# Two neighbouring rows of w_down per partition, and transposes that read every second column

## The chip, the cores and the metric

The kernel runs on one core of a Trainium2 chip. The metric is the device time of one execution in microseconds (us). Engines are named as the profile names them: PE is TensorE's matmul stream and PEld its weight loads, DVE is VectorE, ACT is ScalarE, POOL is GpSimd, SP is SyncE, which here only issues transfers.

## The reference, cut to what matters

The block takes 512 tokens of width 1024 through a mixer (differential attention beside gated linear attention), a cross attention over 256 memory rows, and a mixture of 32 experts with 4 experts a token. All data are float32. The change touches the experts alone:

```python
def expert_block(args):
    xb, e = args
    u = xb @ w_up[e] + b_up[e]
    glu = jnp.minimum(u[:, :D_FF], SWIGLU_LIMIT)
    lin = jnp.clip(u[:, D_FF:], -SWIGLU_LIMIT, SWIGLU_LIMIT)
    act = glu * jax.nn.sigmoid(SWIGLU_ALPHA * glu) * (lin + 1.0)
    return act @ w_down[e] + b_down[e]
```

`D_FF` is 1024, so `w_up[e]` is 1024 x 2048 (8 MB) and `w_down[e]` is 1024 x 1024 (4 MB). The product with `w_down` is a sum over 1024 rows, and its order is free.

## The kernel before

The dense stages come first (a list of steps, `plan_steps`), then the 32 experts. An expert works on up to 96 token slots: group A of 64 and group B of 32. Token rows are gathered from HBM by POOL (lines 530 and 533), transposed by `rows_T` (lines 803 and 805), multiplied with `w_up` in `up_pair` (line 835), put through SwiGLU by DVE and ACT (`swiglu`, `gates`), transposed again by `hidden_T` (lines 813 and 816), multiplied with `w_down` in `down` (line 863 for group A, line 872 for group B), and added to the output rows in HBM by two scatters of POOL (lines 541 and 547).

**Weights.** Every weight goes through `ring`, six slots of 1 MB (8 KB on each of the 128 partitions). SP alone fills it, in a fixed order: in the loop over experts `load_up` issues the eight chunks of the next expert's `w_up`, then `load_down` the four chunks of this expert's `w_down`. A slot is refilled when PE has counted `chunk_used` up for the chunk that it held. Chunk c of `w_up` is rows 128c to 128c+127, row 128c+p on partition p: 8 KB in one piece. Chunk c of `w_down` is two blocks of 128 rows, row 256c+p and row 256c+128+p on partition p: two pieces of 4 KB that lie 512 KB apart in HBM. `down` reads the chunk as two halves, `u` = 0 and 1, each with the transposed activations of index k = 2c+u as weights.

**Activations.** `actA` and `actB` hold the SwiGLU result, 512 columns on each partition. A slot's first 512 features are on one partition and its last 512 on another, so a transpose of 128 columns gives two of the eight indices k. `hidden_T` takes 128 neighbouring columns at a time, as the stationary operand of the transpose (the identity is streamed), into PSUM banks 5 and 6; from there ACT (line 1103) and DVE (line 1473) copy them into `hTA` and `hTB`.

**Order.** PE's order in the loop body of expert i is fixed by the code: the bias of the next expert's up projection (line 824), its chunks 0 and 1, `hidden_T(i)`, `index`, chunks 2 to 7, `rows_T(i+2)`, `down(i)`. Two experts are thus always under way, and DVE and ACT do SwiGLU beside `down`.

Of the kernel before, what the change touches and what calls it, by code (L numbers as in the profile page):

```python
# [14 lines left out]
P = 128  # L15
# [86 lines left out]
def decoder_block(nc, A, slots=SLOTS):  # L102
# [33 lines left out]
    with ExitStack() as ctx:  # L136
        def sb(name, shape, dt=F32):
            return ctx.enter_context(nc.sbuf_tensor(name, shape, dt))

        def sem(name):  # L140
            return ctx.enter_context(nc.semaphore(name))

        bank = [ctx.enter_context(nc.psum_tensor(f"bank{b}", [P, 512], F32)) for b in range(8)]
# [3 lines left out]
        ring_flat = ring.rearrange("p s k n -> p s (k n)")  # L147
# [12 lines left out]
        ident = sb("ident", [P, P])  # L160
# [79 lines left out]
        assert at[0] <= at_gla  # L240
        actT_w = actT.rearrange("p k n -> p (k n)")
        gluA, linA, sigA, actA, gluB, linB, sigB, actB = [actT_w[:, HD * q:HD * q + HD] for q in range(8)]

        sp = [0]

# [24 lines left out]
        chunk_in = [sem(f"chunk_in{s}") for s in range(RING)]  # L270
# [61 lines left out]
        def ps(job):  # L332
            return bank[job_at[job][0]]
# [9 lines left out]
        def ready(eng, job):  # L343
            b, k = job_at[job]
            eng.wait_ge(bank_full[b], k + 1)
# [31 lines left out]
        def up_chunk(e, c):  # L377
            return A["w_up"][0][e, P * c:P * c + P, :]

        def down_chunk(e, c):  # L380
            return A["w_down"][0].rearrange("e (k p) n -> e p k n", p=P)[e, :, 2 * c:2 * c + 2, :]

        slot_dense = [16 * len(range(s, DENSE, RING)) for s in range(RING)]
        def expert_chunk_in(eng, q, o):
# [10 lines left out]
        @block.sync  # L395
        def _(sp_):
            chunk = 0
            for name, g in groups:
                for half in range(2):
                    src = A["w_in"] if name in first_col else A[square[name]]  # L400
                    c0 = first_col[name] if name in first_col else 512 * g
                    if chunk >= RING:
                        ready(sp_, group_jobs[groups[(chunk - RING) // 2]])
                    w = src[0].rearrange("(k p) n -> p k n", p=P)[:, 4 * half:4 * half + 4, c0:c0 + 512]
                    sp_.dma_start(ring[:, chunk % RING, :, :], w).then_inc(chunk_in[chunk % RING], 16)
                    chunk += 1
            ready(sp_, group_jobs[groups[-1]])
            sp_.sem_inc(chunk_used, RING)

            def load_up(q, o, e):  # L410
                for c in range(UP_CHUNKS):
                    sp_.wait_ge(chunk_used, q * PER_EXPERT + (o + c + 1))
                    slot = (o + c) % RING
                    sp_.dma_start(ring_flat[:, slot, :], up_chunk(e, c)).then_inc(chunk_in[slot], 16)

            def load_down(q, o, e):
                for c in range(DOWN_CHUNKS):
                    sp_.wait_ge(chunk_used, q * PER_EXPERT + (o + c + 1))
                    slot = (o + c) % RING
                    sp_.dma_start(ring_flat[:, slot, :].rearrange("p (k n) -> p k n", k=2), down_chunk(e, c)).then_inc(chunk_in[slot], 16)  # L420

            load_up(0, 0, 0)
            with sp_.Fori(0, NE - 1) as i:
                load_up(i, UP_CHUNKS, i + 1)
                load_down(i, UP_CHUNKS + UP_CHUNKS, i)
            load_down(NE - 1, UP_CHUNKS, NE - 1)
            sp_.wait_ge(table_ready, 1)
            extra = sp_.value_load(ovf[0:1, 2 * MO:2 * MO + 1], min_val=0, max_val=MO)
            with sp_.If(extra > 0):
                with sp_.Fori(0, extra) as m:  # L430
                    e = sp_.value_load(ovf[0:1, bass.ds(m, 1)], min_val=0, max_val=NE - 1)
                    load_up(m + NE, 0, e)
                    load_down(m + NE, UP_CHUNKS, e)
            for b in range(NB):
                sp_.wait_ge(fin_ready, b + 1)
                sp_.dma_start(A["out"][0, P * b:P * b + P, :], x_res[:, b, :]).then_inc(out_done, 16)
            sp_.wait_ge(out_done, 16 * NB)
# [139 lines left out]
        def _(pe):  # L577
# [38 lines left out]
            for s in steps:  # L616
# [7 lines left out]
                elif kind == "norm":  # L624
                    n = NORMS[s[1]][0]
                    pe.wait_ge(xn_ready, NB * (n + 1))
                    for k in range(KT):
                        begin(pe, s + (k,))
                        for b in range(NB):
                            t = pe.transpose(ps(s + (k,))[:, P * b:P * b + P], tokA[:, b, P * k:P * k + P], ident[:, :])  # L630
                        finish(t, s + (k,))
                elif kind == "norm_mem":
                    pe.wait_ge(memn_ready, MB)
                    for k in range(0, KT, 2):
                        begin(pe, s + (k,))
                        for k2 in range(2):
                            for b in range(MB):
                                t = pe.transpose(ps(s + (k,))[:, M * k2 + P * b:M * k2 + P * b + P],
                                                 mem_x[:, b, P * (k + k2):P * (k + k2) + P], ident[:, :])
# [5 lines left out]
                elif kind == "qkT":  # L645
                    pe.wait_ge(roped, s[1] + 1)
                    begin(pe, s)
                    for b in range(NB):
                        c0 = 512 * s[1] + P * s[2]
                        t = pe.transpose(ps(s)[:, P * b:P * b + P], tokA[:, b, c0:c0 + P], ident[:, :])  # L650
# [11 lines left out]
                elif kind == "scores":  # L662
                    h, i = s[1] // 4, s[1] % 4
# [7 lines left out]
                elif kind == "attnT":  # L671
                    n, i = s[1], s[1] % 4
                    pe.wait_ge(a_ready, n + 1)
                    begin(pe, s)
                    for j in range(i + 1):
                        t = pe.transpose(ps(s)[:, P * j:P * j + P], abuf[:, n % 2, P * j:P * j + P], ident[:, :])
                    finish(t, s)
                elif kind == "attnV":
                    n, h, i = s[1], s[1] // 4, s[1] % 4
# [7 lines left out]
                elif kind == "gla_scores":  # L687
                    c, t = s[1], s[2]
# [9 lines left out]
                elif kind == "gla_kd":  # L698
                    c, t = s[1], s[2]
                    begin(pe, s)  # L700
                    finish(pe.transpose(ps(s)[:, 0:P], gqkT[:, 2 + t, P * c:P * c + P], ident[:, :]), s)
                elif kind == "gla_out":
                    c, t = s[1], s[2]
# [15 lines left out]
                elif kind == "gla_state":  # L719
                    c, t = s[1], s[2]  # L720
# [4 lines left out]
                elif kind == "oT":  # L725
                    pe.wait_ge(mixed_ready, NB)
                    for k in range(KT):
                        begin(pe, s + (k,))
                        for b in range(NB):
                            t = pe.transpose(ps(s + (k,))[:, P * b:P * b + P], tokA[:, b, P * k:P * k + P], ident[:, :])  # L730
                        finish(t, s + (k,))
                elif kind == "xscores":
                    h, i = s[1], s[2]
# [7 lines left out]
                elif kind == "xT":  # L741
# [3 lines left out]
                    for i in range(NB):  # L745
                        t = pe.transpose(ps(s)[:, P * i:P * i + P], xp[:, h % 2, i, P * mb:P * mb + P], ident[:, :])
# [11 lines left out]
                elif kind == "router":  # L758
# [10 lines left out]
                    for b in range(NB):  # L769
                        t = pe.transpose(ps(j)[:, NE * b:NE * b + NE], lgT[:, P * b:P * b + P], ident[0:NE, 0:NE])  # L770
# [37 lines left out]
            def hidden_T(n):  # L808

                pe.wait_ge(actA_ready, n + 1)  # L810
                pe.wait_ge(actB_ready, n + 1)
                for i in range(KT // 2):
                    t = pe.transpose(bank[5][:, P * i:P * i + P], actA[:, P * i:P * i + P], ident[:, :])  # L813
                t.then_inc(hTA_done, 1)
                for i in range(KT // 2):
                    t = pe.transpose(bank[6][:, 64 * i:64 * i + 64], actB[0:64, P * i:P * i + P], ident[0:64, 0:64])  # L816
                t.then_inc(hTB_done, 1)

            def up_bias(n):
# [68 lines left out]
            with pe.Fori(0, NE - 1) as i:  # L888
                up_bias(i + 1)
                pe.wait_ge(xTA_ready, i + 2)  # L890
                pe.wait_ge(xTB_ready, i + 2)
                up_pair(i, UP_CHUNKS, 0)
                hidden_T(i)
                pe.wait_ge(idx_ready, 2 * i + 4)
                index(i + 2, i + 2)
                for pair in range(1, KT // 2):
                    up_pair(i, UP_CHUNKS, pair)
                pe.wait_ge(hTA_ready, i + 1)
                pe.wait_ge(hTB_ready, i + 1)
                rows_T(i + 2)  # L900
                down(i, i, 2 * UP_CHUNKS)
            pe.wait_ge(xTA_ready, NE + 1)
            pe.wait_ge(xTB_ready, NE + 1)
            hidden_T(NE - 1)
            down(NE - 1, NE - 1, UP_CHUNKS)
            pe.wait_ge(table_ready, 1)
            extra = pe.value_load(ovf[0:1, 2 * MO:2 * MO + 1], min_val=0, max_val=MO)
            with pe.If(extra > 0):
                with pe.Fori(0, extra) as m:
                    e = pe.value_load(ovf[0:1, bass.ds(m, 1)], min_val=0, max_val=NE - 1)  # L910
                    index(m + (NE + 1), e)
                    rows_T(m + (NE + 1))
                    up_bias(m + NE)
                    pe.wait_ge(xTA_ready, m + (NE + 2))
                    pe.wait_ge(xTB_ready, m + (NE + 2))
                    for pair in range(KT // 2):
                        up_pair(m + NE, 0, pair)
                    hidden_T(m + NE)
                    down(m + NE, m + NE, UP_CHUNKS)
# [658 lines left out]
```

## Time and profile before

| | us |
|---|---|
| median of 3 runs | 1800.74 (1798.44 to 1803.96) |
| profiled execution | 1798.54 |
| its span, first to last instruction | 1796.7 |
| dense stages and router, to about 640 | 640 |
| start of the first expert, to 727 | 87 |
| experts at a steady pace, 727 to 1749 | 1022 |
| last product, scatters, final norm, output | 48 |
| mean granted clock of PE, share of full speed | 0.965 |

The span is what the trace shows; the profiled execution took 1.8 us more around it. Busy shares over the whole span mix stages with different limits, so the views below are read by stretch. PE's ends are modelled from a pipeline: a row's mean duration overlaps with its neighbours, and the pace of PE is read from the chain of waits.

### The profile page before, as it was taken

What the parts mean: (1) busy time and instruction counts of PE and PEld (TensorE: products, weight loads), DVE (VectorE), ACT (ScalarE), POOL (GpSimd) and SP (SyncE); (2) the same over time, 40 slices, a digit from 0 to 9 for tenths busy, and PEclk for the clock granted to TensorE, in tenths of its full rate; (3) what the DMA queues carried; (4) which work ended last, traced back from release to release, by engine and by line L of the source; (5) the groups of instructions that cost most, each with busy time, mean ns of one, the idle gap of its engine ahead of it and who ended that gap; (6) DMA issues with size and microseconds to landing.
All of it is one profiled execution on the core that took longest, in us unless ns stands there. A gap on an engine that the chain in (4) does not pass through costs nothing.

```text
span 1796.7 us, 31195 instructions
## 1 busy us (share of the span) xinstructions
PE 1632.7 (91%) x12187; PEld 743.7 (41%) x12188; DVE 533.8 (30%) x1388; ACT 283.1 (16%) x561; POOL 211.4 (12%) x202
## 2 busy tenths in 40 slices
PE   3995979978999758999999999999999999999992
PEld 2442437543454313444434434444443443444441
DVE  2012464221031243223224223323322422322331
ACT  3013324211130201001101101100100110110113
POOL 1000000051000110111121121121111112112111
PEclk9998989989999879999999999999999999999996
DMA  6121111223100557999999999999999999999993
GB/s 213 47 94 47 47 47 48 94 77 105 47 1 0 228 185 309 367 380 387 379 355 401 382 364 390 385 369 384 381 376 381 377 394 364 389 389 369 390 360 107
DMA packets 105522, 467.49 MB, mean 260 GB/s; under 512 B 14062, under 2 KB 14114, under 8 KB 72624
## 3 DMA queue, kind: packets, MB, share of 16 engines
q1 hardware_dynamic: 89152, 438.33, 62.2%
q0 software_dynamic: 13744, 25.46, 5.9%
q10 hardware_dynamic: 2592, 3.25, 0.5%
q8 instruction: 20, 0.33, 0.1%
q14 instruction: 14, 0.11, 0.0%
HBM read 456.89 MB, written 18.87 MB: 265 GB/s over the span
## 4 chain that ended last, share of the span: by engine, by line
PE 86%; DVE 6%; ACT 4%; issue 2%; ACTq 1%; DMA 1%; POOL 0%; DVEq 0%; POOLq 0%
PE bank L835 37%; PE bank L613 20%; PE bank L863 12%; PE bank L872 6%; PE bank L824 1%; PE bank L803 1%; PE bank L813 1%; PE bank L755 1%; DVE arena L1269 1%; PE bank L630 1%; PE bank L805 1%; PE bank L816 1%; ACT L945 1%; PE bank L850 1%; ACT L946 1%
## 5 line engine op out<-in xcount | busy, mean ns | idle before, releaser
L835 PE MATMUL bank<-ring,arena 128*32 128x512 f32 x6144 | 679.2, 594 | 0.0
L835 PEld LDWEIGHTS bank<-ring,arena 128*32 128x32 f32 x6144 | 227.7, 110 | 402.6 <-issue 335.5
L863 PE MATMUL bank<-ring,arena 128*32 128x512 f32 x2048 | 267.8, 592 | 0.0
L613 PE MATMUL bank<-ring,actT 128*128 128x512 f32 x576 | 252.0, 597 | 1.9 <-DVEq L355 1.9
L1450 DVE TENSOR_SCALAR actT<-bank 64x512 f32<-64x512 f32 x64 | 43.7, 683 | 435.1 <-PE bank L835 434.1
L613 PEld LDWEIGHTS bank<-ring,actT 128*128 128x128 f32 x576 | 109.3, 192 | 137.7 <-issue 134.5
L872 PE MATMUL bank<-ring,arena 128*32 128x512 f32 x1024 | 157.9, 592 | 0.0
L863 PEld LDWEIGHTS bank<-ring,arena 128*32 128x32 f32 x2048 | 112.8, 110 | 96.2
L530 POOL DMA_INDIRECT arena<-h_rows,arena x33 | 35.1, 1062 | 901.3 <-DVE arena L1434 901.3
L1097 ACT ACTIVATE actT<-actT 128x512 f32<-128x512 f32 x32 | 20.2, 630 | 526.2 <-DVE actT L1450 526.2
L613 PE MATMUL bank<-actT,ring 128*128 128x512 f32 x192 | 82.8, 593 | 1.2 <-DVEq L355 1.2
L872 PEld LDWEIGHTS bank<-ring,arena 128*32 128x32 f32 x1024 | 58.1, 110 | 51.7
L1480 DVE SCALAR_TENSOR_TENSOR arena<-bank,arena 64x512 f32<-64x512 f32 x32 | 23.8, 743 | 152.0 <-ACT arena L1111 152.0
L1109 ACT ACTIVATE arena<-bank,arena 128x512 f32<-128x512 f32 x32 | 22.0, 687 | 230.6 <-PE bank L863 230.6
L1473 DVE COPY arena<-bank 128x256 f32<-128x256 f32 x32 | 13.5, 423 | 150.6 <-PE bank L816 150.6
L541 POOL DMA_INDIRECT acc_rows<-arena x32 | 51.7, 1615 | 40.4 <-ACT arena L1109 20.0
L613 PEld LDWEIGHTS bank<-actT,ring 128*128 128x128 f32 x192 | 36.4, 190 | 46.9 <-issue 45.4
L547 POOL DMA_INDIRECT acc_rows<-arena x32 | 46.6, 1457 | 9.8 <-issue 9.8
L1103 ACT ACTIVATE arena<-bank 128x512 f32<-128x512 f32 x32 | 19.1, 597 | 178.0 <-PE bank L813 178.0
L630 PE MATMUL bank<-ident,tokA 128*128 128x128 f32 x96 | 16.7, 356 | 31.4 <-DVE tokA L1169 21.1
L1452 DVE TENSOR_SCALAR actT<-bank 64x512 f32<-64x512 f32 x64 | 44.4, 694 | 1.4
L493 POOL DMA_DIRECT2D abuf<-in_w_router x1 | 1.1, 1067 | 368.9 <-DVE tokA L1336 368.9
(284 smaller groups left out, 1308.8 us busy)
## 6 DMA issues: line engine op xcount, KB each, us to landing
ring<-in_w_up SPq DMA_DIRECT2D x256, 1024.0 KB, 6.5
ring<-in_w_down SPq DMA_DIRECT2D x128, 1024.0 KB, 7.8
ring<-in_w_in SPq DMA_DIRECT2D x12, 1024.0 KB, 8.2
ring<-in_w_ck SPq DMA_DIRECT2D x4, 1024.0 KB, 5.6
ring<-in_w_cv SPq DMA_DIRECT2D x4, 1024.0 KB, 6.2
ring<-in_w_out SPq DMA_DIRECT2D x4, 1024.0 KB, 5.7
ring<-in_w_cq SPq DMA_DIRECT2D x4, 1024.0 KB, 6.1
ring<-in_w_co SPq DMA_DIRECT2D x4, 1024.0 KB, 6.3
```

Source lines behind the costliest of these rows:

```text
L530: g.indirect_dma_start(out=xgA[:, :], out_offset=None, in_=h_rows, in_offset=bass.IndirectOffsetOnAxis(ap=idxA_next[:, :], axis=0), bounds ...
L541: g.indirect_dma_start(out=acc_rows, in_=yA[:, :], out_offset=bass.IndirectOffsetOnAxis(ap=idxA_cur[:, :], axis=0), in_offset=None, bounds ...
L547: g.indirect_dma_start(out=acc_rows, in_=yB[0:2 * NARROW, :], out_offset=bass.IndirectOffsetOnAxis(ap=idxB_cur[0:2 * NARROW, :], axis=0), ...
L613: mm = pe.matmul(o, lhsT, rhs, start=(k == 0), stop=(k == KT - 1))
L630: t = pe.transpose(ps(s + (k,))[:, P * b:P * b + P], tokA[:, b, P * k:P * k + P], ident[:, :])
L835: mm = pe.matmul(bank[g][32 * t:32 * t + 32, :], lhsT, w[:, 512 * t:512 * t + 512], start=False, stop=(k == KT - 1))
L863: mm = pe.matmul(bank[3][r:r + 32, :], hTA[:, k % 4, g, k // 4, :], w[:, 512 * t:512 * t + 512], start=False, stop=(k == KT - 1))
L872: mm = pe.matmul(bank[4][r:r + 32, :], hTB[:, k % 4, k // 4, :], w[:, 512 * t:512 * t + 512], start=(k == 1), stop=(k >= KT - 2))
L1109: a.activation(yA, bank[3][:, :], ACT.Copy, scale=gateA_tab[:, bass.ds(col, 1)]).then_inc(yA_ready, 1)
L1450: v.tensor_scalar(gluA[64 * g:64 * g + 64, :], bank[g][0:64, :], LIMIT, None, ALU.min).then_inc(gluA_ready, 1)
L1452: ins = v.tensor_scalar(linA[64 * g:64 * g + 64, :], bank[g][64:128, :], LIMIT, -LIMIT, ALU.min, ALU.max)
L1480: v.scalar_tensor_tensor(out=yB[0:64, :], in0=bank[4][0:64, :], scalar=gateB_tab[0:64, bass.ds(col, 1)], in1=yB_odd[0:64, :], op0=ALU.mult ...
```

## The change

Two things change together. First, chunk c of `w_down` becomes rows 256c to 256c+255 with rows 256c+2p and 256c+2p+1 on partition p. These lie next to each other in HBM, so each partition's 8 KB is one piece, and the transfer's pattern is 128 x 2048 in place of 128 x 2 x 1024. The slot's half `u` then holds the rows 256c+2p+u. Second, the transposes of `hidden_T` must bring the matching features to partition p: index k = 2c+u now needs features 256c+2n+u for n from 0 to 127, which are every second column of a block of 256. The view `actA_u` names them; transpose i reads block i // 2, parity i % 2, with a step of two columns (8 bytes). What the transposes write, the copies after them and the loops of `down` are as they were. No instruction is added, removed or moved on any engine: the five engines' programs have as many rows as before, in the same order.

```diff
         gluA, linA, sigA, actA, gluB, linB, sigB, actB = [actT_w[:, HD * q:HD * q + HD] for q in range(8)]
+        actA_u, actB_u = [t_.rearrange("p (c n u) -> p c n u", n=P, u=2) for t_ in (actA, actB)]
...
         def down_chunk(e, c):
-            return A["w_down"][0].rearrange("e (k p) n -> e p k n", p=P)[e, :, 2 * c:2 * c + 2, :]
+            return A["w_down"][0].rearrange("e (c p u) n -> e c p (u n)", p=P, u=2)[e, c, :, :]
...
                     slot = (o + c) % RING
-                    sp_.dma_start(ring_flat[:, slot, :].rearrange("p (k n) -> p k n", k=2), down_chunk(e, c)).then_inc(chunk_in[slot], 16)
+                    sp_.dma_start(ring_flat[:, slot, :], down_chunk(e, c)).then_inc(chunk_in[slot], 16)
...
                 for i in range(KT // 2):
-                    t = pe.transpose(bank[5][:, P * i:P * i + P], actA[:, P * i:P * i + P], ident[:, :])
+                    t = pe.transpose(bank[5][:, P * i:P * i + P], actA_u[:, i // 2, :, i % 2], ident[:, :])
                 t.then_inc(hTA_done, 1)
                 for i in range(KT // 2):
-                    t = pe.transpose(bank[6][:, 64 * i:64 * i + 64], actB[0:64, P * i:P * i + P], ident[0:64, 0:64])
+                    t = pe.transpose(bank[6][:, 64 * i:64 * i + 64], actB_u[0:64, i // 2, :, i % 2], ident[0:64, 0:64])
                 t.then_inc(hTB_done, 1)
```

## Rows read from the trace of the kernel before

**Rows 1.** Busy time by stretch: us, then engines, granted clock, DMA share, GB/s.

```profile
0.00:640.00 640.00, 524.37 (x1611) 273.36 (x1612) 177.63 (x432) 146.05 (x343) 42.80 (x68) 0.94 0.22 77
640.00:727.00 87.00, 74.24 (x686) 27.71 (x690) 29.39 (x94) 7.93 (x12) 8.52 (x9) 0.89 0.74 283
727.00:1749.00 1022.00, 1022.00 (x9784) 436.21 (x9776) 319.43 (x854) 109.75 (x178) 151.86 (x118) 1.00 0.99 380
1749.00:1797.00 48.00, 12.11 (x114) 6.44 (x110) 7.33 (x10) 19.37 (x29) 8.27 (x8) 0.66 0.33 103
```

**Rows 2.** All that PE waited for from 645: total us, times, longest.

```profile
PE bank L824 <- DVE arena L1442: 6.1, 1, 6.1
PE bank L803 <- DMA arena<-h_rows,arena: 6.1, 1, 6.1
PE bank L850 <- DVE arena L1473: 1.2, 1, 1.2
```

**Rows 3.** SP's waits from 645, and SP's issues around 1000 (start, us).

```profile
SPq L420 <- PE bank L835: 287.6, 126, 3.3
SPq L414 <- PE bank L872: 286.5, 120, 3.5
...
1000.97 8.09 SPq L420 DMA_DIRECT2D ring<-in_w_down  x4
1011.29 20.54 SPq L414 DMA_DIRECT2D ring<-in_w_up  x8
1035.43 8.09 SPq L420 DMA_DIRECT2D ring<-in_w_down  x4
```

**Rows 4.** Chain of waits inside one expert's body: start, us, what ran.

```profile
893.39 0.58 PE bank L813 x4
893.98 0.39 PE bank L816 x4
894.37 0.19 PE bank L794 x4
894.55 0.10 PE bank L796 x4
894.65 15.59 PE bank L835 x144
...
927.85 0.59 PE bank L813 x4
```

**Rows 5.** Transfers to landing: the page's medians; L420 alone, 727 to 1700.

```profile
ring<-in_w_up SPq DMA_DIRECT2D x256, 1024.0 KB, 6.5
ring<-in_w_down SPq DMA_DIRECT2D x128, 1024.0 KB, 7.8
...
DMA to landing us min/median/max: 5.6/7.8/9.9
```

**Rows 6.** Packets over the whole span, from the page.

```profile
DMA packets 105522, 467.49 MB, mean 260 GB/s; under 512 B 14062, under 2 KB 14114, under 8 KB 72624
q1 hardware_dynamic: 89152, 438.33, 62.2%
```

**Rows 7.** Packets of queue q1 (SP): 1010.5 to 1013.5, then 1016 to 1022.

```profile
q1 hardware_dynamic: 323, 1.25, 102.0%
...
q1 hardware_dynamic: 343, 2.55, 101.7%
```

**Rows 8.** Lines 813, 816, 613: duration in ns, min/median/max, and shapes.

```profile
L813 PEld LDWEIGHTS bank<-ident,actT x128: 137/140/145, 686.5 to 1749.4; 128*128 128x128 f32 x128
L816 PEld LDWEIGHTS bank<-ident,actT x128: 135/138/141, 687.1 to 1749.9; 64*128 64x128 f32 x128
L613 PEld LDWEIGHTS bank<-ring,arena x64: 186/190/192, 324.5 to 358.8; 128*128 128x128 f32 x64
```

**Rows 9.** Passes of 512 columns: dense stage (line 613), experts (line 835).

```profile
L613 PE MATMUL bank<-ring,actT x576: 592/592/1057, 35.2 to 601.5; 128*128 128x512 f32 x192
L835 PE MATMUL bank<-ring,arena x6144: 591/592/1062, 650.2 to 1736.8; 128*32 128x512 f32 x199
```

## The prediction

> **What bounds the kernel now.** I read the busy time by stretch first, because the change lies wholly in the expert loop. From 727 to 1749 PE is busy for 1022.00 of 1022.00 us at the full granted clock (1.00, the 2.4 GHz level) [rows 1]. In the same stretch the DMA engines are at a share of 0.99 and move 380 GB/s. So two resources look full, and the question for this change, which helps one of them, is which one sets the pace.
>
> The waits answer it. From 645 on PE waited three times in all, 6.1, 6.1 and 1.2 us, for a weight selector, for the first gather of token rows, and for one copy of transposed activations at the very end [rows 2]. Not one wait is on a chunk of the ring, so PE never stood still for a weight. The other side of the ring tells the same: SP waits for PE 126 times before a `w_down` chunk (287.6 us) and 120 times before a `w_up` chunk behind `down` (286.5 us) [rows 3]. It is the full ring that holds SP back. The pace confirms it: SP's four `w_down` issues begin at 1000.97 and the next four at 1035.43, a period of 34.46 us [rows 3], and the transposes of line 813 begin at 893.39 and at 927.85 in the chain of waits, again 34.46 us [rows 4]. Both follow PE's own list of instructions. The DMA share of 0.99 says that packets are under way, not that anybody waits for them.
>
> **The margin of a chunk.** A slot is freed when PE ends a chunk and is needed again six chunks later, so at least five chunks of PE work lie between. Six chunks of the up projection take 15.59 us in the chain [rows 4], 2.60 each, so five are 13.0 us. `w_down` chunks land after 7.8 us at the median and 9.9 us at the worst [rows 5]. The worst one still has 3.1 us to spare, the typical one 5.2 us.
>
> **Part one, the transfers.** 128 transfers change (32 experts, 4 chunks). In each, 256 packets of 4 KB become 128 of 8 KB. That takes 128 x 128 = 16384 packets off queue q1, which had 89152, and off the total of 105522; the packets under 8 KB, 72624 of them, lose all 32768 of `w_down` [rows 6].
>
> What a packet costs I take from two stretches in which q1 moves nearly one kind only. From 1010.5 to 1013.5 it moves 1.25 MB, 305 pieces of 4 KB, at a share of 102.0% of 16 engines x 3 us: 49.0 us, or 160 ns a piece. From 1016 to 1022 it moves 2.55 MB, 311 pieces of 8 KB, at 101.7% of 96 us: 97.6 us, or 314 ns [rows 7]. Two small ones cost 320 ns, one large one 314: 6 ns gained. An engine gets 8 of the large pieces of a chunk, so a chunk saves about 50 ns and the kernel 128 x 8 x 6 ns = 6.1 us of DMA time. Bounds: none of it, or all of it. All of it would need the DMA to set the pace; it does not [rows 2, 3]. A landing of 7.8 us that became 7.7, or even the 6.5 us of `w_up` [rows 5], is further inside a margin that is never used. I take 0 us. The cover is PE's own work, 34.46 us for an expert. It is not thick: the twelve chunks of an expert take each DMA engine 64 pieces of 314 ns and 64 of 160 ns, 30.3 us, and the gathers and scatters come on top. If PE were some 3 us an expert faster, the 6.1 us would begin to count.
>
> The Trainium skill, Perfetto Trace Analysis, section DMA Optimizations, says that larger transfers saturate HBM better and can "dramatically improve throughput", from 2 KB to 4 or 8 KB, and ties this to a kernel that is DMA-bound. By that rule, with its condition left aside, this would be a gain. The packets of rows 7 differ by 2% per byte, and the condition is not met.
>
> Could the new pattern be slower? `w_up` is fetched today with just this pattern, 128 x 2048 with 8 KB a partition and 1 MB in one piece, and lands sooner, at 6.5 us [rows 5]. That excludes a loss worth a term. The issue itself, on SP, lies in a wait for PE. The gathers and scatters share the engines with this queue, and nothing in the steady loop waits for them [rows 2].
>
> **Part two, the transposes.** 8 transposes an expert now load a stationary operand whose columns stand 8 bytes apart: 256 loads in all, 128 on line 813 and 128 on line 816 [rows 8]. These lie on the path, since PE is the bound. The writes to PSUM and the copies behind them are unchanged.
>
> No row of this trace shows a strided load by PE, so the cost is bounded. First, how much of a load is on the path? Four transposes of line 813 take 0.58 us in the chain and four of line 816 0.39 us [rows 4], 145 and 98 ns each. They differ by 64 streamed columns, so 64 columns are worth 47 ns and 128 columns 94 ns. Some 50 ns of each transpose is thus not streaming; it is of the kind that a slower load would lengthen. So I do not count on a hidden load: what a load grows by, PE loses.
>
> The lower bound is 0: each load stays at 140 ns and 138 ns. I see no way below zero, as no column is saved. A middle value is the slower kind of load of the same shape that the trace has: 128x128 float32 for an ordinary matmul takes 190 ns against 140 for the transposes [rows 8], 50 ns more. 256 x 50 ns = 12.8 us. The upper bound is a load that doubles outright: 256 x 139 ns = 35.6 us. I take 0 us. The nearest rows are those of the same loads; the operand has the same number of columns and the same partitions, and each is a single 4-byte word per partition either way.
>
> The Trainium skill, Advanced Engine Details and Errata, section Memory Cachelines, says that SBUF is read in lines of 16 bytes and that at least two accesses must hit a line to hide the memory's latency. At 8 bytes apart two of the wanted words lie in each line where four did, so by that rule the cost is nothing, but this is its last free step; if the rule were off by one hit, the slower case below would hold. No run here shows it yet.
>
> **The sum.** Transfers 0, transposes 0, everything else untouched: 1798.5 us for an execution like the profiled one (span 1796.7 and 1.8 around it). That execution was 2.2 us under the median of the three runs, and nothing in the change removes that spread, so the forecast for the median is the median before, 1800.7 us.
>
> **The rivals.**
>
> *Strided loads cost (slower).* The place is lines 813 and 816; the price is the growth of a load times 256. Against it: same column count. For it: no strided load in the trace, and loads that are not hidden. With the middle value it gives 1800.7 + 12.8 = 1813.5 us, with the upper bound 1836.3 us. It is decisive from 21 ns a load (5.4 us, 0.3%).
>
> *The DMA is the bound after all (faster).* For it: the share of 0.99. Against it: no wait of PE on the ring. A second way to gain would be that DMA writes slow PE's reads; but a pass of 512 columns takes 592 ns in the dense stage, at a DMA share of 0.22, and 592 ns among the experts at 0.99 [rows 1, 9]. In full this rival gives 1800.7 - 6.1 = 1794.6 us.
>
> *The packets do not change.* If the pattern were cut into 4 KB pieces anyway, the count on q1 would stay at 89152, and the time would still be 1800.7 us, since the transfers are hidden. `w_up` speaks against it: the packets of 8 KB and over are 105522 - 72624 = 32898 [rows 6], which is 256 x 128 of `w_up` and a few more.
>
> **How the numbers follow.** Forecast (with the packets changed) 0.74; packets unchanged, same time, 0.03; strided loads at about 50 ns 0.12; strided loads nearer to doubling 0.05, which leaves a little for loads that grow by less than 21 ns in the first case; DMA gain 0.06. Within 0.3% is about what a measurement of this kernel can tell from no change, 5.4 us here. That gives faster 0.05 (the DMA gain's price is just past the limit, so a part of it stays within), same 0.78, slower 0.17. The range goes from the DMA gain, 1794.6, to the middle price of the strided loads, 1813.5 with half a microsecond for scatter; it leaves out the doubling and half of what lies around 1813.5.
>
> **What the profile after would show.** Right: q1 at 72768 packets (89152 - 16384), packets under 8 KB at 39856 (72624 - 32768), loads of lines 813 and 816 still at 140 and 138 ns, the four transposes at 0.58 and 0.39 us in the chain, the period of SP's `w_down` issues at 34.46 us, no wait of PE on the ring, `w_down` landing between 6.5 and 7.8 us. Wrong on the slow side: loads of 813 and 816 at 160 ns or more, and a period longer by eight times the growth, 0.40 us at 50 ns. Wrong on the fast side: a period under 34.46 us with the same PE instructions, which would mean that PE's pace hung on the DMA in a way that the waits do not show.

## The result: 10 us slower, all of it in the transposes

The changed kernel takes 1809.33 us (median of 7 runs, 1807.85 to 1814.31); the kernel before, timed beside it, takes 1799.13 us (7 runs, 1798.3 to 1804.09). The ratio is 1.0056 with a 95% interval from 1.0039 to 1.0073: slower, by 10.2 us. The time lies inside the range that was given, but the forecast was no change, and that was wrong.

The stretches of the kernel after, as in [rows 1]:

```profile
0.00:640.00 640.00, 530.24 (x1611) 277.37 (x1612) 173.51 (x412) 146.16 (x343) 41.71 (x65) 0.94 0.22 77
640.00:727.00 87.00, 69.14 (x630) 26.23 (x630) 32.22 (x104) 7.33 (x11) 7.74 (x9) 0.86 0.69 263
727.00:1749.00 1022.00, 1022.00 (x9700) 442.20 (x9702) 313.69 (x850) 108.25 (x175) 153.99 (x120) 1.00 0.98 376
1749.00:1812.00 63.00, 27.54 (x256) 13.72 (x248) 14.58 (x23) 21.60 (x32) 8.28 (x8) 0.74 0.48 174
```

PE is still busy for all of the steady stretch, at the full clock, but it gets through 9700 instructions where it did 9784 [rows 1]. It has become slower at its own work; nothing has come to stand in its way. What it waited for from 645 on, as in [rows 2], names no chunk of the ring. The wait of 7.1 us is not new: the kernel before has it too (7.13 us, ending at 640.5), and here it falls behind 645 because this execution is some 5 us later at that point. SP waits for PE before `w_down` chunks a little longer than before (302.0 us against 287.6, [rows 3]):

```profile
PE bank L795 <- DVE arena L1421: 7.1, 1, 7.1
PE bank L825 <- DVE arena L1443: 6.2, 1, 6.2
PE bank L804 <- DMA arena<-h_rows,arena: 6.1, 1, 6.1
PE bank L851 <- DVE arena L1474: 0.8, 1, 0.8
...
SPq L421 <- PE bank L836: 302.0, 126, 3.6
```

The lines after 240 stand one higher than before: 814 and 817 are the transposes of `hidden_T`, 804 and 806 those of `rows_T`, 836 is the up projection. SP's issues give the period (start, us), and the chain of waits through one body (start, us, what ran) gives the place, to be laid beside [rows 3] and [rows 4]:

```profile
904.95 8.05 SPq L421 DMA_DIRECT2D ring<-in_w_down  x4
...
939.74 8.05 SPq L421 DMA_DIRECT2D ring<-in_w_down  x4
```

```profile
900.44 0.68 PE bank L814 x4
901.12 0.62 PE bank L817 x4
901.74 0.19 PE bank L795 x4
901.93 0.10 PE bank L797 x4
902.03 15.59 PE bank L836 x144
917.62 0.59 PE bank L804 x4
918.21 0.39 PE bank L806 x4
```

The period is 34.79 us in place of 34.46, 0.33 us more. The four transposes of group A went from 0.58 to 0.68 us and the four of group B from 0.39 to 0.62, which is 0.33 us too. The up projection is at 15.59 us as before, and the transposes of `rows_T`, which were not touched, at 0.59 and 0.39. 32 experts times 0.33 us are 10.6 us; 10.2 were measured. Thirty periods together, from SP's first group of `w_down` issues to its 31st, took 1033.95 us before (690.79 to 1724.74) and 1043.61 us after (696.23 to 1739.84): 9.66 us more, 0.322 a period, 10.3 us in 32 experts. The weight loads behind it, as in [rows 8] (ns, min/median/max):

```profile
L814 PEld LDWEIGHTS bank<-ident,actT x128: 194/209/223, 691.6 to 1764.6; 128*128 128x128 f32 x128
L817 PEld LDWEIGHTS bank<-ident,actT x128: 191/213/220, 692.3 to 1765.3; 64*128 64x128 f32 x128
...
L804 PEld LDWEIGHTS bank<-ident,arena x132: 138/140/230, 652.1 to 1752.7; 128*128 128x128 f32 x132
```

The strided loads take 209 and 213 ns where they took 140 and 138; the loads of line 804 stay at 140. The other half of the change did what it says (packets, as in [rows 6], and landings, as in [rows 5]):

```profile
DMA packets 89139, 467.49 MB, mean 258 GB/s; under 512 B 14063, under 2 KB 14115, under 8 KB 39857
q1 hardware_dynamic: 72768, 438.33, 61.7%
...
ring<-in_w_up SPq DMA_DIRECT2D x256, 1024.0 KB, 6.8
ring<-in_w_down SPq DMA_DIRECT2D x128, 1024.0 KB, 7.0
```

The profiled execution of the kernel after, 1813.64 us, is 15.1 us over the profiled one of before. Some 5 us of that lie ahead of the experts: line 804 begins at 652.1 us, line 803 of before at 647.0. PE's granted clock differs there (from 170 to 300 it is 0.88 of full speed after, 0.91 before), and executions of either kernel differ by so much among themselves, 1798.3 to 1804.1 us before and 1807.9 to 1814.3 after. The experiments are therefore read by the period in the steady stretch, and their medians beside it.

### The profile page after: what moved, and what is told of

Read it like the earlier page. It is cut to its first block, busy times and chain, and to the rows that moved or that the text cites. A ratio compares the mean times of both kernels' runs of the same rounds, so it can differ in the third digit from the quotient of the medians.

```text
span 1811.9 us, 31195 instructions
## 1 busy us (share of the span) xinstructions
PE 1648.9 (91%) x12187; PEld 759.5 (42%) x12188; DVE 534.0 (29%) x1388; ACT 283.3 (16%) x561; POOL 211.7 (12%) x202
## 2 busy tenths in 40 slices
DMA packets 89139, 467.49 MB, mean 258 GB/s; under 512 B 14063, under 2 KB 14115, under 8 KB 39857
## 3 DMA queue, kind: packets, MB, share of 16 engines
q1 hardware_dynamic: 72768, 438.33, 61.7%
## 4 chain that ended last, share of the span: by engine, by line
PE 86%; DVE 6%; ACT 4%; issue 2%; ACTq 1%; DMA 1%; POOL 0%; DVEq 0%; POOLq 0%
PE bank L836 37%; PE bank L614 20%; PE bank L864 12%; PE bank L873 6%; PE bank L825 1%; PE bank L814 1%; PE bank L804 1%; PE bank L817 1%; PE bank L756 1%; PE bank L631 1%; DVE arena L1270 1%; PE bank L806 1%; ACT L946 1%; PE bank L851 1%; ACT L947 1%
```

## The experiments

Two theories stood after the result. Theory L: the strided weight loads are the whole loss. Rival D: the 8 KB pieces cost something, with the longer loads only beside it. The first four kernels undo one part each, move the cost to another engine, and double it. "The kernel before" ran beside each set.

### The transfers alone

```diff
# against the changed kernel
-                    t = pe.transpose(bank[5][:, P * i:P * i + P], actA_u[:, i // 2, :, i % 2], ident[:, :])
+                    t = pe.transpose(bank[5][:, P * i:P * i + P], actA[:, P * i:P * i + P], ident[:, :])
...
-                    t = pe.transpose(bank[6][:, 64 * i:64 * i + 64], actB_u[0:64, i // 2, :, i % 2], ident[0:64, 0:64])
+                    t = pe.transpose(bank[6][:, 64 * i:64 * i + 64], actB[0:64, P * i:P * i + P], ident[0:64, 0:64])
```

> Only the transfers change: each partition's 8 KB of a w_down chunk is one piece, the transposes read neighbouring columns as before. (The features meet the wrong rows of w_down, so the sum over the 1024 features is paired wrongly; the work is the same.) Theory L, the strided weight loads are the whole loss: the time of before, 1799 us within 3, a period of 34.46 us for SP's w_down issues, no wait of PE on the ring, w_down landing at about 7.0 us in place of 7.8. Rival D, the 8 KB pieces disturb something (gathers, the dense stages that ended 5 us later in the profile after): about 1809 us, with lines 813 and 816 at 140 and 138 ns.

1799.37 us against 1799.38, ratio 1.0004 (0.9995 to 1.0014). The `w_down` issues start 34.47 us apart here, and thirty periods take 1033.94 us where the kernel before took 1033.95:

```profile
828.70 8.05 SPq L421 DMA_DIRECT2D ring<-in_w_down  x4
...
863.17 8.05 SPq L421 DMA_DIRECT2D ring<-in_w_down  x4
```

The loads of both lines are back at 140 and 138 ns. The 8 KB pieces cost nothing and bring nothing here. One item of the expectation missed: `w_down` landed after 8.5 us at the median (5.2 to 10.4), not sooner than the 7.8 of before. Even 10.4 us is under the 13 us after which the slot is read.

### The strided transposes alone

```diff
# against the kernel before
+        actA_u, actB_u = [t_.rearrange("p (c n u) -> p c n u", n=P, u=2) for t_ in (actA, actB)]
...
-                    t = pe.transpose(bank[5][:, P * i:P * i + P], actA[:, P * i:P * i + P], ident[:, :])
+                    t = pe.transpose(bank[5][:, P * i:P * i + P], actA_u[:, i // 2, :, i % 2], ident[:, :])
...
-                    t = pe.transpose(bank[6][:, 64 * i:64 * i + 64], actB[0:64, P * i:P * i + P], ident[0:64, 0:64])
+                    t = pe.transpose(bank[6][:, 64 * i:64 * i + 64], actB_u[0:64, i // 2, :, i % 2], ident[0:64, 0:64])
```

> Only the transposes change: they read every second column, the transfers are two pieces of 4 KB as before. (The features meet the wrong rows of w_down; the work is the same.) Theory L: the time of after, 1809.5 us within 3; weight loads of the two transposes at about 209 and 213 ns, four transposes at 0.68 and 0.62 us in the chain, a period of 34.79 us. Rival D: 1799 us.

1810.29 us against 1799.38, ratio 1.0059 (1.0044 to 1.0074). The period is 34.79 us (832.53 to 867.32 in SP's issues), the chain has 0.68 and 0.62 us for the two fours. The whole loss is here, with the old transfers. Theory L holds and rival D falls.

### The same pairing with the step moved to DVE

```diff
# against the changed kernel
-        actA_u, actB_u = [t_.rearrange("p (c n u) -> p c n u", n=P, u=2) for t_ in (actA, actB)]
+        actA_o, actB_o = [t_.rearrange("p (c u n) -> p c u n", n=P, u=2) for t_ in (actA, actB)]
+        linA_u, sigA_u, linB_u, sigB_u = [t_.rearrange("p (c n u) -> p c u n", n=P, u=2) for t_ in (linA, sigA, linB, sigB)]
...
-                v.tensor_tensor(actA, linA, sigA, ALU.mult).then_inc(actA_ready, 1)
+                v.tensor_tensor(actA_o, linA_u, sigA_u, ALU.mult).then_inc(actA_ready, 1)
...
-                v.tensor_tensor(actB[0:64, :], linB[0:64, :], sigB[0:64, :], ALU.mult).then_inc(actB_ready, 1)
+                v.tensor_tensor(actB_o[0:64], linB_u[0:64], sigB_u[0:64], ALU.mult).then_inc(actB_ready, 1)
```

The transposes read `actA` and `actB` 128 neighbouring columns at a time again.

> The whole change, but DVE's last product of SwiGLU reads its operands with a step of two columns and writes them in the order that the transposes want, so that every weight load reads neighbouring columns. The result is that of the changed kernel. Theory L: 1799 us within 3, the period back at 34.46 us, DVE's two products perhaps longer than 0.69 us (a step of 8 bytes) but hidden, since actB is ready about 10 us before hidden_T. Rival D: 1809 us. If DVE's strided reads doubled its two products, the 1.4 us an expert would still be hidden.

1800.0 us against 1799.38, ratio 1.0006 (0.9996 to 1.0017): this kernel computes what the changed kernel computes, with its 8 KB pieces, in the time of the kernel before. DVE's groups by shape (busy us, mean ns):

```profile
L1464 DVE TENSOR_TENSOR actT<-actT 128x512 f32<-128x512 f32 x32 | 23.9, 748 | 1.1
L1471 DVE TENSOR_TENSOR actT<-actT 64x512 f32<-64x512 f32 x32 | 23.4, 730 | 0.0
```

The two products, which read both operands with a step of two columns, take 748 and 730 ns. In the kernel before the same two products (lines 1462 and 1469) took 692 and 673 ns. DVE pays 56 and 57 ns for 512 columns, once each an expert, on an engine that is not the bound.

### The suspected cost doubled

```diff
# against the changed kernel
+        xgA_u, xgB_u = [t_.rearrange("p (c n u) -> p c n u", n=P, u=2) for t_ in (xgA, xgB)]
...
-                    pe.transpose(bank[5][:, P * i:P * i + P], xgA[:, P * i:P * i + P], ident[:, :])
+                    pe.transpose(bank[5][:, P * i:P * i + P], xgA_u[:, i // 2, :, i % 2], ident[:, :])
...
-                    t = pe.transpose(bank[6][:, 64 * i:64 * i + 64], xgB[0:64, P * i:P * i + P], ident[0:64, 0:64])
+                    t = pe.transpose(bank[6][:, 64 * i:64 * i + 64], xgB_u[0:64, i // 2, :, i % 2], ident[0:64, 0:64])
```

> The suspected cost doubled: the changed kernel, whose transposes of the gathered token rows (rows_T, lines 804 and 806 of the changed kernel) also read every second column. (The token features then meet the wrong rows of w_up; the work is the same.) Theory L: another 0.33 us an expert, 1.0 to 1.1 us for the 33 pairs in all 10.8 us more than the changed kernel: about 1820 us, 21 us over the kernel before, loads of lines 804 and 806 (here one line lower) at about 209 and 213 ns. Rival D: no more than the changed kernel, 1809 us.

1824.2 us against 1799.38 (4 runs, 1820.57 to 1826.44), ratio 1.0131 (1.0112 to 1.0151): 24.8 us over the kernel before where 21 were expected. The period is 35.11 us (812.64 to 847.75 in SP's `w_up` issues), 0.65 over 34.46, which is twice 0.33 and makes 20.8 us in 32 experts. Where the remaining 4 us between the medians lie is not shown. The profiled execution reaches the first transposes of token rows at 653.7 us, 6.7 later than the profiled one of before, and this later start does not come with the step: the kernels with steps of three and four columns, further down, issue their first `w_down` chunk at 691.5 and 691.9 us, the kernel before at 690.8. The fastest runs of the two kernels are 22.7 us apart.

### One group at a time, and wider steps

The load grew by about 70 ns, but a transpose of group A only by about 23 and one of group B by about 58. Two kernels take the step away from one group each.

```diff
# stride_a, against the changed kernel: only group B's transposes are put back
-                    t = pe.transpose(bank[6][:, 64 * i:64 * i + 64], actB_u[0:64, i // 2, :, i % 2], ident[0:64, 0:64])
+                    t = pe.transpose(bank[6][:, 64 * i:64 * i + 64], actB[0:64, P * i:P * i + P], ident[0:64, 0:64])
```

> Only the four transposes of group A (128 streamed columns) read every second column, those of group B read neighbours. (Group B's features meet the wrong rows of w_down; the work is the same.) Theory C, the stream covers a part of a longer load: the load grows by 69 ns but the transpose by 24 to 26 only, four of them 0.68 us in place of 0.59, a period of 34.55 us, about 3 us over the kernel before. Rival S, each group's growth came partly from the other group's loads queued beside it: the four A transposes and the four B transposes would then share 0.33 us in another way, and this kernel would cost about half of it, 5 us.

> Only the four transposes of group B (64 streamed columns) read every second column. (Group A's features meet the wrong rows of w_down; the work is the same.) Theory C: four of them 0.62 us in place of 0.39, a period of 34.69 us, about 7.5 us over the kernel before. Rival S: about 5 us.

The second kernel puts back group A's in the same way. The chains of the two, A's first:

```profile
929.33 0.68 PE bank L814 x4
930.01 0.39 PE bank L817 x4
```

```profile
929.82 0.59 PE bank L814 x4
930.41 0.62 PE bank L817 x4
```

With A alone the period is 34.56 us (829.93 to 864.49) and the median 1802.23 us, ratio 1.0007 (0.9996 to 1.0018); with B alone 34.70 us (830.15 to 864.85) and 1808.59 us, 1.0040 (1.0025 to 1.0056). For A alone the medians do not tell a loss from none; the periods do. Thirty of them take 1036.65 us with A alone and 1040.90 with B alone, 2.70 and 6.95 us over the kernel before, and 9.65 together, where the changed kernel lost 9.66. Each group has its own growth, whatever the other does, so rival S falls. The parts are 0.09 and 0.23 us an expert.

The group with half the streamed columns loses more than twice as much. The likely reason, theory C, is that its stream is too short to cover the load: with the step a transpose takes 170 ns in group A and 155 in group B, 15 ns apart, where 47 ns lay between them before. But group B's operand also covers 64 partitions in place of 128 (64x128 against 128x128 in the rows of the loads), and no run changes one without the other. So the size of each part is shown, and its reason is argued.

Two more kernels widen the step, to three and to four columns:

```diff
# stride_four, against the changed kernel; stride_three has u=3 over the first 384 columns and set i % 3
-        actA_u, actB_u = [t_.rearrange("p (c n u) -> p c n u", n=P, u=2) for t_ in (actA, actB)]
+        actA_u, actB_u = [t_.rearrange("p (n u) -> p n u", u=4) for t_ in (actA, actB)]
...
-                    t = pe.transpose(bank[5][:, P * i:P * i + P], actA_u[:, i // 2, :, i % 2], ident[:, :])
+                    t = pe.transpose(bank[5][:, P * i:P * i + P], actA_u[:, :, i], ident[:, :])
...
-                    t = pe.transpose(bank[6][:, 64 * i:64 * i + 64], actB_u[0:64, i // 2, :, i % 2], ident[0:64, 0:64])
+                    t = pe.transpose(bank[6][:, 64 * i:64 * i + 64], actB_u[0:64, :, i], ident[0:64, 0:64])
```

> The changed kernel with a step of three columns (12 bytes) in place of two; the four transposes of a group read three sets of 128 columns, the first of them twice. (Features 384 to 511 of each half are left out and the others are paired wrongly; the work is the same.) Theory U, any step above one column puts the load at one slower rate: loads at about 210 ns and the time of the changed kernel, 1809.5 us. Theory G, a load costs by how far it reaches in the partition (512 bytes with neighbours, 1024 with step two, 1536 here): another 70 ns a load, about 280 ns, and 256 x 70 = 18 us more, since the stream has nothing left to cover: 1827 us.

> The changed kernel with a step of four columns (16 bytes): transpose i reads every fourth column from column i. (The features are paired wrongly with the rows of w_down; the work is the same.) Theory U: 1809.5 us, loads at about 210 ns. Theory G: loads at about 350 ns and 2 x 18 us over the changed kernel, 1845 us.

The loads, step three first, then step four (ns, min/median/max):

```profile
L814 PEld LDWEIGHTS bank<-ident,actT x128: 188/200/218, 687.0 to 1758.9; 128*128 128x128 f32 x128
L817 PEld LDWEIGHTS bank<-ident,actT x128: 187/210/213, 687.6 to 1759.5; 64*128 64x128 f32 x128
```

```profile
L814 PEld LDWEIGHTS bank<-ident,actT x128: 195/210/220, 687.3 to 1760.2; 128*128 128x128 f32 x128
L817 PEld LDWEIGHTS bank<-ident,actT x128: 191/216/217, 687.9 to 1760.9; 64*128 64x128 f32 x128
```

1811.5 us (1.0059, 1.0036 to 1.0083) and 1811.1 us (1.0058, 1.0039 to 1.0078): the time of step two. Theory G falls. Theory U holds nearly: thirty periods lose 8.63 us at step three (0.29 a period) and 9.64 at step four (0.32), against 9.66 at step two. Neighbours and not neighbours is the difference that counts, and step three is even a little cheaper.

### The cover of the transfers taken away

The prediction put the gain of the transfers at 6.1 us that PE hides. Two kernels with less work for PE show it in the open.

```diff
# thin_4k, against the kernel before
-                    for g in range(3):
+                    for g in range(3 if k >= KT - 2 else 2):
...
-                    for u in range(2):
+                    for u in range(2 if c == DOWN_CHUNKS - 1 else 0):
...
-                                           start=(k == 1), stop=(k >= KT - 2))
+                                           start=(k == KT - 1), stop=(k >= KT - 2))
```

The middle edit is in the second of the two loops over `u` in `down`, that of group B. thin_8k makes the same edits to the kernel with the transfers alone.

> The cover taken away: the kernel before with less work for PE. Group B's products are left out for the first six of eight chunks of w_up and the first three of four of w_down (so group B's results are not the reference's). PE then needs 34.46 - 6 x 0.86 - 3 x 0.86 = 26.7 us an expert, under the 30.3 us that its twelve chunks take each DMA engine, gathers and scatters on top. Both theories: the DMA sets the pace, PE waits on the ring, a period of about 32.5 us, about 1737 us in all. It is the reference for thin_8k.

> thin_4k with the 8 KB pieces and transposes of neighbouring columns. Theory P, the gain is what the packets showed (320 ns for two small ones, 314 for one large one): 0.19 us an expert, 6.1 us in all, about 1731 us. Rival G: fewer packets also let the small packets of gathers and scatters through sooner, or the other way round, and the gain is 1 us an expert and more, 32 us in all, about 1705 us. Rival N: no gain at all.

Here PE does wait for the ring (total us, times, longest, 660 to 1700; 4 KB pieces first):

```profile
PE bank L835 <- DMA ring<-in_w_up: 97.9, 111, 2.4
PE bank L863 <- DMA ring<-in_w_down: 23.9, 41, 0.8
```

```profile
PE bank L836 <- DMA ring<-in_w_up: 94.6, 108, 2.2
PE bank L864 <- DMA ring<-in_w_down: 16.6, 34, 0.6
```

and SP's `w_down` issues give the periods; the pair shown has 32.06 us and 31.71 us:

```profile
869.52 7.20 SPq L420 DMA_DIRECT2D ring<-in_w_down  x4
...
901.58 7.18 SPq L420 DMA_DIRECT2D ring<-in_w_down  x4
```

```profile
868.70 7.15 SPq L421 DMA_DIRECT2D ring<-in_w_down  x4
...
900.41 7.14 SPq L421 DMA_DIRECT2D ring<-in_w_down  x4
```

The medians are 1725.45 us (ratio to the kernel before 0.9587, 0.9571 to 0.9604) and 1714.24 us (0.9528, 0.9509 to 0.9547). The periods are not even here, 31.4 to 33.6 us, so a mean over many tells more than a pair. From 740.85 to 1616.74 us thin_4k runs 27 periods of 32.44 us, and thin_8k from 741.34 to 1608.90 us 27 periods of 32.13 us. The larger pieces are worth 0.31 us an expert when the DMA sets the pace, 9.9 us in 32 experts; the medians are 11.2 us apart and the profiled executions 9.3. That is more than the 6.1 us of theory P and far from the 32 us of rival G.

The packets of SP's queue from 727 to 1600 us show the same (packets, MB, share of 16 engines; 4 KB pieces first):

```profile
q1 hardware_dynamic: 60524, 339.96, 95.4%
...
q1 hardware_dynamic: 47141, 343.31, 95.0%
```

16 engines x 873 us x the share are 39.2 us of engine time for one MB with the 4 KB pieces and 38.7 with the 8 KB ones. Over the 12.6 MB of an expert and its 512 pairs of pieces that is some 13 ns a pair, where the prediction had read 6 ns. So the packets' own time is enough to explain the gain.

The period of thin_4k came as estimated, 32.44 us against about 32.5, but the two times came out 12 to 17 us under those expected. Much of that lies ahead of the steady stretch, which the estimate had left as it was: thin_4k issues its first `w_down` chunk at 683.28 us, the kernel before at 690.79.

### Does a streamed operand pay for a step?

```diff
# against the kernel before
-                            mm = pe.matmul(bank[4][r:r + 32, :], hTB[:, k % 4, k // 4, :], w[:, 512 * t:512 * t + 512],
+                            mm = pe.matmul(bank[4][r:r + 32, :], hTB[:, k % 4, k // 4, :], w.rearrange("p (n v) -> p n v", v=2)[:, :, t],
```

> Does the streamed operand pay for a step too? The kernel before, in which group B's products with w_down stream every second column of the chunk (a step of 8 bytes; the output columns come out interleaved, so the result is not the reference's). Theory W, only weight loads pay: 1799 us, eight passes still 0.86 us in the chain. Rival B, a step costs any operand: passes that double would add 4 x 0.86 us an expert, 110 us in all.

1807.1 us, ratio 1.0032 (1.0017 to 1.0047). Neither theory is right. Eight passes take 0.90 to 0.92 us in the chain in place of 0.86, and a pass alone 618 ns at the median where the kernel before has 592:

```profile
918.18 1.72 PE bank L863 x16
919.90 0.92 PE bank L872 x8
920.82 1.72 PE bank L863 x16
922.54 0.91 PE bank L872 x8
...
L872 PE MATMUL bank<-ring,arena x1024: 609/618/647, 711.1 to 1774.6; 128*32 128x512 f32 x171
```

A streamed operand with a step of two pays as well, 4 to 7% of its passes here, far from a doubling. The four groups of eight in an expert make 0.22 us, 7 us in 32 experts; the medians are 6.4 us apart.

## Why the prediction was wrong, point by point

**PE is the bound, and no wait is on the ring.** Right. The kernel after shows the same, and thin_4k shows what it looks like when it is not so.

**Part one, the transfers, 0 us.** Right: the transfers alone gave 1.0004 (0.9995 to 1.0014). The packet counts came out as said, 72768 on q1, and 39857 under 8 KB where 39856 had been worked out. The price behind the cover, 6.1 us, was too small; without the cover 10 to 11 us came out. It was read from two short stretches, where the difference is 6 ns in 320; over 873 us with the DMA as the bound it is some 13 ns. And where PE is the bound it does not show at all: from 727 to 1700 us queue q1 was at 91.8% for 354.66 MB before and at 92.1% for 354.56 MB with the transfers alone. The time of a packet is thus no constant that can be carried from one state of the queue to another. The landing was not a good witness either: 7.0 us at the median in the kernel after, but 8.5 with the transfers alone.

**Part two, the transposes, 0 us.** This is the step that failed: the term for the transposes, put at 0 us in the sum, measured 10.3 us by the periods and 10.2 by the medians. The prediction had no row for a strided load, bounded its cost between 0 and 35.6 us, and then took the lower end "by the nearest rows", which were the same loads without a step. Those rows say nothing of a step. The load grew from 140 to 209 ns and from 138 to 213. The middle value, 50 ns from the slower kind of load in [rows 8], was nearer.

**"What a load grows by, PE loses."** Also wrong, in the other direction. 128 x 69 + 128 x 75 ns would have been 18.4 us; the path lost 10.3. In group A some 23 ns of 69 reach the path, in group B some 58 of 75. The reading of the chain, 50 ns of each transpose that is not streaming, compared two groups that differ in partitions as well as in streamed columns, and even if it is right for the loads of before, it does not follow that a longer load is wholly exposed. The rival's 1813.5 us came within 4.2 us of the measured 1809.33 by luck: a growth taken too small, 50 ns, and an exposure taken too large went against each other, 12.8 us for the 10.3 of the periods.

**The rule on lines of 16 bytes.** The Trainium skill, Advanced Engine Details and Errata, section Memory Cachelines, was read as "no cost at a step of two". The traces do not agree: in the kernel after, step two has two words in a line and costs 69 to 75 ns a load. Step four (stride_four) has one word in a line and costs no more, 210 and 216 ns in all. Nor was step two free for the streamed operand (592 to 618 ns a pass) or for DVE (692 to 748 ns a product). The measurement decides: for these loads the count of hits in a line does not set the cost. The prediction gave the slower rival a chance of 0.17; what stood against that rival was the unchanged count of columns and this rule, and no row with a step spoke for either.

**The DMA rival and the packets that do not change.** Both fell, as expected: the transfers alone moved nothing, and the count on q1 fell by 16384. The Trainium skill, Perfetto Trace Analysis, section DMA Optimizations, ties the gain of larger transfers to a DMA-bound kernel. The runs agree with the condition: 1.0004 where PE is the bound, 11.2 us of 1725.45 where the DMA is. From 4 to 8 KB the gain is small even there, for the third of the bytes that changed.

**Signs to look for.** The period was named as the sign, longer by eight times the growth of a load. It showed the sign at once, though not by that multiple: 8 times 72 ns would be 0.58 us, and 0.33 came.

## What to carry to other kernels

Price both halves of a layout change by who is the bound. Here the half that gains sits behind PE and the half that costs sits on PE, so even a small cost decides; when a step must go somewhere, put it on an engine with time to spare, as DVE had (1.0006 in place of 1.0056). Where the trace has no row for an operation on the bound engine, zero is a bound and not an estimate.

## What the runs showed of the hardware that was not expected

- A weight load of 128 float32 columns for a transpose takes 140 ns with neighbouring columns and 200 to 216 ns with a step of two, three or four; wider is not slower in that range.
- Only a part of that reaches the path, and not the same part: four transposes with 128 streamed columns (128 partitions) went from 0.59 to 0.68 us, four with 64 (64 partitions) from 0.39 to 0.62.
- A streamed float32 operand with a step of two made eight passes of 512 columns take 0.90 to 0.92 us in place of 0.86. A DVE product of 128x512 float32 with both inputs at a step of two took 748 ns in place of 692.
- Two 4 KB pieces in place of one of 8 KB cost 0.31 us in 4 MB when the DMA sets the pace (a mean period of 32.44 us against 32.13), about 1%.

Open is why the rate is nearly the same for two, three and four columns, whether the streamed columns or the partitions decide how much of a load is covered, and whether a step costs the loads of ordinary matmuls as much. No run here tries them.
